# Neighbourhood attention: half of the probability maps turned by VectorE and sixteen on-chip transfers instead of TensorE

## The reference, cut to what matters

```python
def _na_mixer(h, hc, w_in, rpb, w_out, need_ctx_out):
    q, k, v, g = jnp.split(h @ w_in, 4, axis=-1)          # q scaled by 64 ** -0.5
    kc, vc = jnp.split(hc @ w_in[:, WIDTH:3 * WIDTH], 2, axis=-1)
    ...
    s_loc = s_loc + bias[None]        # rpb[:, dr, dc], 16 columns around each query, all 4 rows
    s_ctx = jnp.einsum('brqhd,bchd->bhrqc', q, kc)
    p = jax.nn.softmax(jnp.concatenate([s_loc.reshape(...), s_ctx], axis=-1), axis=-1)
    ...
    o = einsum(p_blk, vb) + einsum(p_ctx, vc)
    y = (o.reshape(b_, l_, WIDTH) * jax.nn.silu(g)) @ w_out
```

## Time and profile before

| | |
|---|---|
| median of three runs | 1814.95 us |
| the profiled execution: own time, span | 1815.61 us, 1813.8 us |
| PE, DVE, ACT, POOL busy, share of the span | 99%, 53%, 50%, 75% |
| granted TensorE clock, mean over the span | 0.998 |
| DMA: bytes, mean rate | 372.91 MB, 206 GB/s |
| busy from 300 to 350 us (attention): PE, DVE, ACT, POOL | 49.99, 33.29, 33.78, 22.94 us |
| DMA share from 300 to 350 us, rate | 0.71, 183 GB/s |

### The profile page before, as it was taken

One profiled execution on the slowest core, in us unless ns is written; L12 is line 12 of the kernel. 1 busy time (PEld: TensorE's weight loads), 2 busy tenths in 40 slices (PEclk: granted clock), 3 DMA queues, 4 the chain that ended last, 5 costly groups with the idle time before them and its releaser, 6 DMA issues.

```text
span 1813.8 us, 24988 instructions
## 1 busy us (share of the span) xinstructions
PE 1793.3 (99%) x9274; PEld 1477.5 (81%) x9274; DVE 954.2 (53%) x1756; ACT 901.5 (50%) x1329; POOL 1366.0 (75%) x568
## 2 busy tenths in 40 slices
PE   6999999999999999999999999999999999999999
PEld 5888888887889888887788888888888878888887
DVE  4673766778755524866653230713095876143152
ACT  3324424674455644456554644464445565555452
POOL 2624544559968898977689798969897867888885
PEclk9999999999999999999999999999999999999999
DMA  9863885749775775565665566567655666656663
GB/s 366 291 210 94 270 310 163 198 141 312 244 277 200 211 221 191 180 198 168 209 186 192 179 195 191 193 187 234 191 193 185 192 190 182 196 160 210 190 195 128
DMA packets 206457, 372.91 MB, mean 206 GB/s; under 512 B 33508, under 2 KB 59092, under 8 KB 205780
## 3 DMA queue, kind: packets, MB, share of 16 engines
q1 hardware_dynamic: 203328, 363.69, 63.5%
q10 hardware_dynamic: 3028, 7.86, 1.2%
HBM read 367.27 MB, written 9.28 MB: 208 GB/s over the span
## 4 chain that ended last, share of the span: by engine, by line
PE 97%; DVE 2%; DMA 0%; issue 0%; ACTq 0%; ACT 0%; POOL 0%; DVEq 0%
PE ps L1300 26%; PE ps L1302 25%; PE ps L1301 25%; PE ps L1426 3%; PE ps L1427 3%; PE ps L1428 3%; PE ps L1992 1%; PE ps L1993 1%; PE ps L1994 1%; PE ps L1348 1%; PE ps L1697 1%; PE ps L1918 1%; PE ps L1668 1%; PE ps L1678 1%; PE ps L1962 1%; PE ps L1558 1%
## 5 line engine op out<-in xcount | busy, mean ns | idle before, releaser
L659 POOL TENSOR_TENSOR w_lo<-raw,w_hi 128x1024 fp32r<-128x1024 f32 x556 | 1347.1, 2461 | 397.4 <-ACT w_hi L697 376.2
L1300 PE MATMUL ps<-w_hi,act_rows_r 128*128 128x512 f32 x2064 | 814.8, 395 | 3.2 <-POOL w_lo L659 3.1
L1302 PE MATMUL ps<-w_hi,act_rows_r 128*128 128x512 f32 x2064 | 805.2, 390 | 0.0
L1301 PE MATMUL ps<-w_lo,act_rows_r 128*128 128x512 f32 x2064 | 804.6, 390 | 0.0
L697 ACT ACTIVATE w_hi<-raw 128x1024 fp32r<-128x1024 f32 x556 | 571.1, 1058 | 371.0 <-DMA raw<-in_ffn_w_up 100.8
L1300 PEld LDWEIGHTS ps<-w_hi,act_rows_r 128*128 128x128 f32 x2064 | 388.2, 188 | 90.4 <-issue 9.1
L1302 PEld LDWEIGHTS ps<-w_hi,act_rows_r 128*128 128x128 f32 x2064 | 388.0, 188 | 82.0
L1301 PEld LDWEIGHTS ps<-w_lo,act_rows_r 128*128 128x128 f32 x2064 | 388.4, 188 | 77.7
L2647 DVE STREAM_TRANSPOSE ps<-proj 32x256 f32<-32x256 f32 (+1 forms) x384 | 166.5, 434 | 6.5
L2628 DVE TENSOR_TENSOR proj<-proj,ps 128x1024 f32<-128x1024 f32 (+1 forms) x18 | 20.4, 1132 | 252.2 <-PE ps L1302 247.9
L1426 PE MATMUL ps<-act_rows_r,w_hi 128*128 128x512 f32 (+1 forms) x288 | 101.3, 352 | 0.0
(11 more groups left out here) (245 smaller groups left out, 1554.0 us busy)
## 6 DMA issues: line engine op xcount, KB each, us to landing
raw<-in_w_in SPq DMA_DIRECT2D x120, 512.0 KB, 3.9
raw<-in_ffn_w_gate SPq DMA_DIRECT2D x88, 512.0 KB, 4.4
raw<-in_ffn_w_up SPq DMA_DIRECT2D x88, 512.0 KB, 4.4
raw<-in_ffn_w_down SPq DMA_DIRECT2D x88, 512.0 KB, 4.2
proj<-in_ada_w SPq DMA_DIRECT2D x39, 512.0 KB, 7.9
pt<-in_ada_w SPq DMA_DIRECT2D x38, 512.0 KB, 6.4
raw<-in_pool_w_in SPq DMA_DIRECT2D x32, 512.0 KB, 7.3
raw<-in_na_w_in SPq DMA_DIRECT2D x32, 512.0 KB, 4.9
```

Of the source, the lines that this page charges most:

```text
L659: pool.tensor_tensor(w_lo[:, s, :], raw[:, s, :], w_hi[:, s, :].bitcast(F32), ALU.subtract).then_inc(lo_done, 1)
L1300: pe.matmul(o, h, hi, start=start, stop=False)
L1301: pe.matmul(o, h, lo, start=False, stop=False)
L1302: return pe.matmul(o, c, hi, start=False, stop=stop)
```

## The change

For the units 0, 2, 4, 6, 8 and 10 (`NA_SQUARED`) PE no longer transposes. DVE transposes the maps inside each 32x32 block (`turned`), and the blocks then still lie on the wrong partitions. `exchange` moves them: sixteen transfers from SBUF to SBUF, each of 32 partitions x 1 KB, eight issued by SP and eight by ACT, from a buffer of squares (in `pt` or `bias`, by turns) to one placed buffer in `proj`. PE waits for all sixteen (`na_placed`), and reads the placed maps in runs of 32 columns. The values of a squared unit come five rounds after its scores instead of three (`na_due`). ACT issues its eight in round u + 4, SP after the output-weight group of that time.

The bias is loaded raw: four DMAs for each pair of heads, each 64 partitions x one run of 219 numbers, into a window buffer in `proj`; POOL reads the overlapping windows, adds the mask and writes the bias where DVE reads it, in two instructions, and waits itself for DVE to have used the earlier bias. The first two pairs are loaded at group 12 of the stage's input weights instead of group 7. The relation tables are written in the first block of each layer's first feed-forward stage.

```diff
+NA_SQUARED = (0, 2, 4, 6, 8, 10)
...
         def na_out_bank(u):
-            return 2 if u < NA_UNITS - 3 else 4
+            return 3 if u == NA_SQUARED[-1] else 2 if u < NA_UNITS - 3 else 4
+        def na_due(i):
+            return [u for u in range(NA_UNITS - 1) if u + (5 if u in NA_SQUARED else 3) == i]
+        def na_placed_rows(dims, at=0, rows=slice(0, P)):
+            return free(proj[rows, 0:1], dims, CTX_RES + 2 * D + at)
+        def na_squares(u, dims, at=0, rows=slice(0, P)):
+            return free((bias if u // 2 % 2 else pt)[rows, 0:1], dims, 2048 * (u // 2 % 2) + at)
+        def exchange(queue, u, targets):
+            queue.wait_ge(dve_done, dve_s.count(("na_sq", u)))
+            if u:
+                queue.wait_ge(pe_done, pe_s.count(("na_out", u - 2)))
+            for kq in targets:
+                for q in range(4):
+                    queue.dma_start(na_placed_rows([[1, 256]], 256 * q, slice(32 * kq, 32 * kq + 32)),
+                                    na_squares(u, [[1, 256]], 256 * kq, slice(32 * q, 32 * q + 32))).then_inc(na_placed, 16)
...
# SP
             def load_bias(hp):
-                for h, t, rq in ((h, t, rq) for h in range(2) for t in range(NT) for rq in range(2)):
-                    src = bass.AP(na_rows.tensor, (2 * hp + h) * RPB_HEAD + (7 - 2 * t - rq) * RPB_C + 15,
-                                  [[NA_ROW - 1, GRID_W], [RPB_C, 4], [1, GRID_W]])
...
+                if hp >= 2:
+                    sp.wait_ge(bias_masked, hp - 1)
+                for h in range(2):
+                    for rq in range(2):
+                        src = bass.AP(na_rows.tensor, (2 * hp + h) * RPB_HEAD + (5 - rq) * RPB_C + 15, [[NA_ROW - 1, GRID_W], [1, RPB_SPAN]])
+                        sp.dma_start(bias_windows(hp, [[1, RPB_SPAN]], h * 256, slice(64 * rq, 64 * rq + 64)), src).then_inc(bias_in[hp % 2], 16)
...
             for j in range(8):
                 if j < 6:
-                    sp.wait_ge(dve_done, dve_s.count(("na_l", 2 * j + 1)))
                     load_bias(j + 2)
                 send(I["na_w_out"][0][j * P:(j + 1) * P, :], [[1, D]])
-                if j in (1, 3):
-                    keep_rel(j // 2)
+                if 2 * j - 2 in NA_SQUARED:
+                    exchange(sp, 2 * j - 2, (0, 1))
+            sp.wait_ge(na_placed, 256 * len(NA_SQUARED))
...
+                        if tables and pair == 0:
+                            keep_rel(l)
...
# POOL
             def masked(hp):
-                pool.wait_ge(bias_in[hp % 2], 128 * (hp // 2 + 1))
-                both = free(bias[:, 0:1], [[SEQ, 4], [1, SEQ]], (hp % 2) * 1024)
-                pool.tensor_tensor(both, both, free(na_mask[:, 0:1], [[0, 4], [1, SEQ]]), ALU.add).then_inc(bias_masked, 1)
+                pool.wait_ge(bias_in[hp % 2], 64 * (hp // 2 + 1))
+                if hp >= 2:
+                    pool.wait_ge(dve_done, dve_s.count(("na_l", 2 * hp - 3)))
+                for t in range(NT):
+                    last = pool.tensor_tensor(free(bias[:, 0:1], [[512, 2], [GRID_W, 4], [1, GRID_W]], (hp % 2) * 1024 + t * SEQ), ...
# ACT, round i
-                        if i >= 3:
+                        if i - 3 in NA_SQUARED:
+                            act.wait_ge(dve_done, dve_s.count(("na_sq", i - 3)))
+                        elif i >= 3:
                             act.wait_ge(pe_done, pe_s.count(("na_t", i - 3, 1)))
...
+                    if i - 4 in NA_SQUARED:
+                        exchange(act, i - 4, (2, 3))
...
+                        if u not in NA_SQUARED:      # the copy of the turned maps, u = i - 2
...
# PE
             def na_values(u):
-                pe.wait_ge(dve_done, dve_s.count(("na_pt", u, 0)))
-                pe.wait_ge(act_done, act_s.count(("na_pt", u, 1)))
+                if u in NA_SQUARED:
+                    pe.wait_ge(na_placed, 256 * (u // 2 + 1))
+                else:
+                    pe.wait_ge(dve_done, dve_s.count(("na_pt", u, 0)))
+                    pe.wait_ge(act_done, act_s.count(("na_pt", u, 1)))
...
+                        maps = na_placed_rows([[256, 4], [1, 32]], 32 * (4 * c + k)) if u in NA_SQUARED else pt[:, o:o + P]
...
-                    if i >= 2:
+                    due = na_due(i)
+                    for u in due[:-1]:
+                        na_values(u)
+                    if i >= 2 and i - 2 not in NA_SQUARED:
                         na_turned(i - 2)
-                    if i >= 3:
-                        na_values(i - 3)
+                    for u in due[-1:]:
+                        na_values(u)
...
# DVE
                 def turned(u):
+                    if u in NA_SQUARED:
+                        dve.wait_ge(act_done, act_s.count(("na_e", u, 1)))
+                        if u >= 4:
+                            dve.wait_ge(na_placed, 256 * (u // 2 - 1))
+                        dve.transpose(na_squares(u, [[32, 8], [256, 4], [1, 32]]),
+                                      na_rows_of(u, [[P, 8], [32, 4], [1, 32]])).then_inc(dve_done, dve_s.one(("na_sq", u)))
+                    else:                            # the copy as before
...
```

More of the change, by code:

```diff
@@ L508, in narrow @@
                                 x_made(sp, prev, 1, nb)
[L509 to L512, removed]
+                        if stage == "na_in" and g == 12:
+                            sp.wait_ge(scratch_in, 16)
+                            load_bias(0)
+                            load_bias(1)
                         if stage == "na_in" and g == 16:
@@ L662, in masked @@
             def masked(hp):
-                pool.wait_ge(bias_in[hp % 2], 128 * (hp // 2 + 1))
-                both = free(bias[:, 0:1], [[SEQ, 4], [1, SEQ]], (hp % 2) * 1024)
-                pool.tensor_tensor(both, both, free(na_mask[:, 0:1], [[0, 4], [1, SEQ]]), ALU.add).then_inc(bias_masked, 1)
+                pool.wait_ge(bias_in[hp % 2], 64 * (hp // 2 + 1))
+                if hp >= 2:
+                    pool.wait_ge(dve_done, dve_s.count(("na_l", 2 * hp - 3)))
+                for t in range(NT):
+                    last = pool.tensor_tensor(free(bias[:, 0:1], [[512, 2], [GRID_W, 4], [1, GRID_W]], (hp % 2) * 1024 + t * SEQ),
+                                              bias_windows(hp, [[256, 2], [RPB_C, 4], [1, GRID_W]], 2 * RPB_C * (1 - t)),
+                                              free(na_mask[:, 0:1], [[0, 2], [GRID_W, 4], [1, GRID_W]]), ALU.add)
+                last.then_inc(bias_masked, 1)
             pool.wait_ge(dve_done, dve_s.count(("first_gains", 0, 1)))
@@ L962, in na_layer @@
                         u = i - 2
[L963 to L967, removed]
+                        if u not in NA_SQUARED:
+                            act.wait_ge(pe_done, pe_s.count(("na_t", u, 1)))
+                            if u == 12:
+                                act.wait_ge(na_placed, 256 * 5)
+                            if u >= 2:
+                                act.wait_ge(pe_done, pe_s.count(("na_out", u - 2)))
+                            act.activation(pt[:, (u % 2) * 1024 + 512:(u % 2) * 1024 + 1024], ps[:, 7, :],
+                                           ACT.Copy).then_inc(act_done, act_s.one(("na_pt", u, 1)))
                         if i == NA_UNITS:
@@ L1696, in na_values @@
                         o = (u % 2) * 1024 + c * 512 + k * P
-                        last = pe.matmul(ps[c * HD:(c + 1) * HD, bank, 0:P], v, pt[:, o:o + P], start=k == 0, stop=k == 3)
+                        maps = na_placed_rows([[256, 4], [1, 32]], 32 * (4 * c + k)) if u in NA_SQUARED else pt[:, o:o + P]
+                        last = pe.matmul(ps[c * HD:(c + 1) * HD, bank, 0:P], v, maps, start=k == 0, stop=k == 3)
                 last.then_inc(pe_done, pe_s.one(("na_out", u)))
@@ L2438, in turned @@
                 def turned(u):
[L2439 to L2442, removed]
+                    if u in NA_SQUARED:
[5 more added lines that the diff above has]
+                    else:
+                        dve.wait_ge(pe_done, pe_s.count(("na_t", u, 0)))
+                        if u == 12:
+                            dve.wait_ge(na_placed, 256 * 5)
+                        if u >= 2:
+                            dve.wait_ge(pe_done, pe_s.count(("na_out", u - 2)))
+                        dve.tensor_copy(pt[:, (u % 2) * 1024:(u % 2) * 1024 + 512], ps[:, 6, :]).then_inc(dve_done, dve_s.one(("na_pt", u, 0)))
                     dve.wait_ge(act_done, act_s.count(("na_e", u, 1)))
@@ L2476, in gated @@
                     dve.wait_ge(pe_done, pe_s.count(("tp", "nag", 0, k)))
[L2477 removed]
+                    dve.wait_ge(dve_done, dve_s.count(("na_o", na_last_of(k))))
                     z = ps[:, NA_Z_BANK[k], :].rearrange("p (c n) -> p c n", c=2)
@@ L2490, in na_layer @@
                         dve.wait_ge(pe_done, pe_s.count(("na_s", i)))
-                        if i >= 3:
+                        if i >= 3 and i - 3 not in NA_SQUARED:
```

(7 more changed lines are left out.)

11 lines of the change are left out of this document (7 added, 4 removed).

## The result

The changed kernel takes 1823.98 us (median; 1822.71 to 1824.72) against 1814.75 us of the kernel before on the same chip: 1.0048 times as long, 95% interval 1.0035 to 1.0060. The forecast was 1811.1 us, faster, in a range of 1809.0 to 1817.0; the kernel came out 9.2 us slower than before, 12.9 us above the forecast. The profiled execution has a span of 1822.6 us where that of before had 1813.8.

The account below looks back on a forecast made before the run. The prediction took TensorE (PE) to bound the kernel, 97% of the span; -5.2 + 0.85 + 0.5 = -3.85 us brought the profiled 1815.61 to 1811.76, by the median 1811.1 us, range 1809.0 to 1817.0.

Parts of the forecast that it names:

- ACT: Step on ACT's queue: eight DMA issues in every even round from 4 to 14, 0.46 us apart, 3.7 us.
- The rest: Step on bias loads, GpSimd's mask, SP's waits and relation copies: nothing added; eight bias loads take 0.65 us of SP each.
- Arrival: Transfers at a squared unit's values: there at 5.85 us after the scores; 0.1 us charged to five units, 0.85 to the first.
- ACT's pair: ACT's work for a pair of units: 0.2 + 3.7 + 1.05 + 2.0 + 0.5 = 7.5 us of 7.95.
- the flight: Time from a transfer's last issue to its landing: 1.8 us, and 0.15 for the semaphore.
- Transposes: On PE, six of sixteen units lose eight transposes: 6 x 0.87 = 5.2 us saved.
- Waits for transfers: PE's waits at squared units' values: 0.85 us in the first and 0.5 over the five others.
- t = 6.0: PE reaches the values waiting for the transfers 6.0 us after the scores of the round four later end.
- DVE's transposition: DVE transposes 128x1024 within 32x32 blocks instead of a 0.68 us copy: 1.30 us by size, between 0.98 and 1.30.
- The third: Rival at PE's values: their wait costs more than the transposes, from a mean stall of 0.87 us; chance 0.09.
- The fourth: Rival on ACT: issues start only after its copy and exponentials; +6.4 us, 1821.3; chance 0.04.
- The fifth: Rival on SP's and ACT's queues: they issue strictly in turn, stall 2.45 us in six units; +9.5, 1824.4; chance 0.02.

Follow-up runs that it names:

- experiment 3: Changed kernel, all transfers made but none waited for; exchanged units' values read a constant matrix instead of the placed maps: 1822.63 us, ratio 1.0049.
- experiment 7: Kernel of experiment 4 with the write of the squares put ahead of the next weight load: 1815.04 us, ratio 0.9996.
- experiment 8: Kernel of experiment 7 with unit 12's copies no longer waiting for unit 10's values: 1812.86 us, ratio 0.9993.
- experiment 9: Kernel of experiment 8 with unit 0 left to TensorE's transposes, so five units exchanged: 1811.59 us, ratio 0.9979.
- experiment 4: Changed kernel with each exchange by way of DRAM, one write and four reads, all issued by SP: 1819.53 us, ratio 1.0023.
- experiment 6: Changed kernel, SP alone moving the squares in four transfers of 128 rows of 1 KB, blocks landing straight: 1815.08 us, ratio 1.0001.
- experiment 1: Changed kernel with no unit exchanged, raw bias runs and moved relation copies kept: 1815.01 us, ratio 1.000.
- experiment 10: Changed kernel, on-chip exchange over two queues kept, without unit 0 and with unit 12's copies freed: 1822.46 us, ratio 1.0035.
- experiment 2: Changed kernel with only SP's eight transfers of each exchange made and waited for, ACT issuing none: 1817.82 us, ratio 1.0022.
- experiment 11: Changed kernel with all sixteen transfers of each exchange issued by SP, none by ACT: 1850.97 us, ratio 1.0188.

## Why the prediction was wrong

**The step that failed** is in "ACT": "twelve issues on ACT's queue, first and last shown, come 0.46 us apart, so eight are 3.7 us". They are 0.6 us apart, and eight take 5.0 to 6.6 us. A row that says so was in the prediction: the bias loads of this very stage, 5.20 us for eight, which the section "The rest" read as 0.65 us each. The start-up issues were taken because they stood on ACT's queue; the engine was not what mattered (592 ns on SP, 614 to 620 on ACT). Why the start-up issues are shorter no run shows. With 5.0 us the prediction's own sums turn over. Arrival: 0.2 + 5.0 + 1.95 = 7.15 against 6.0, a stall of 1.15 in five units and 2.15 in the first, 7.9 us. ACT's pair: 0.2 + 5.0 + 1.05 + 2.0 + 0.5 = 8.75 us, more than the 7.95 it had. Both consequences are shown, the second by experiment 3. That 7.9 lies near the measured 6.8 is in part luck: the flight was too long in the sum (with 1.3 us in place of 1.95 a regular row gives a stall of 0.5, and unit 8 has 0.52), and two rows were longer than 5.3 us by single long issues, which the prediction had no term for.

**Two terms stood at nothing without a row.** That moving unit 10's values back by two rounds holds up unit 12's copies, which wait for them, is nowhere in the prediction; it cost 2.5 us (experiments 7 and 8). And the scores of round 4 were brought forward by 1.9 us without asking whether DVE's sums come forward too: they did not; PE waits 0.5 us there, and 0.2 us at a query tile before.

**The sum, term by term.** Transposes: -5.2 forecast, borne out (0.87 a unit in experiment 9). Waits for transfers: +1.35 forecast, +6.8 measured. Ends of the stage, not in the sum: +3.2. Clock after the long wait, not in the sum: +1.4. Small waits for DVE: +0.4. Together +6.6; the stage measured +7.5, and 0.9 us is not assigned, with eleven waits in the stage. The same remainder is 0.8, 0.8, 0.4 and 0.3 us in experiments 3, 4, 6 and 8, with nine, nine, four and two waits, so it seems to go with their number; what it is was not traced.

**What held.** The place and time at which PE asks (t = 6.0), DVE's transposition (1.23 us, inside 0.98 to 1.30), that bias runs and relation copies are about free (experiment 1; five other profiles, the changed kernel's and those of experiments 6, 7, 8 and 10, have a wait of 0.4 to 0.7 us for weights in the first feed-forward stage, two of them before the first relation copy is issued; its cause was not traced), and that ACT's first issues run beside its exponentials. The value products' reading in runs of 32 columns cost nothing: sixteen take 1.09 us at full clock, as in the earlier trace rows.

**The rivals.** The third, the price nearest to the truth in kind (values wait more than the transposes cost), "decides from a mean stall of 0.87 us"; the mean stall was 1.1, but it came from the issues, where the rival has a flight of some 2.6 us. The fourth, issues that start only behind ACT's copy and exponentials, is refuted: the first starts at 327.42, 0.1 us after the scores. What it comes near to is another thing, ACT's own later work held behind the last five issues. The fifth, two queues strictly in turn, is refuted by experiment 2 and by the rows after: each queue keeps 0.6 us while the other issues. The Trainium skill (Perfetto Trace Analysis, "DMA Instruction — HWDGE (DVE, Sync)") has an exclusive lock there; no run here shows one at this cadence.

**Rule and row on the issues.** The Trainium skill (DMA: Bandwidth & Descriptors, "Issuing engines are not separate DMA queues") says that the time to initiate a DMA is "usually small relative to the DMA itself". Here it is not: of the 1.9 us from issue to landing 0.6 are the issue, and eight issues take 5.0 us, 2.6 times as long as one transfer from issue to landing.

## What to carry to other kernels

Count a transfer's issue as an instruction of its engine, with a duration read from issues of the same stage and in a row, before its bytes or its flight: here a few large transfers beat many small ones, and the engine that computes on the path is better off issuing none. Where a buffer's last reader is moved later, list everything that waits on that reader's semaphore. When a queue carries a transfer on the path, put it ahead of the bulk load that nothing waits for yet.

## What the runs showed of the hardware

- The length of an issue hardly depends on its bytes: 32 rows of 1 KB 0.59 us, 128 rows of 1 KB 0.60 us. The placing from DRAM, 32 rows of four runs, took 0.43 us, and the 512 KB write 0.34 to 0.38 (experiments 4 and 8).
- Single issues take 1.2 to 2.1 us now and then, on either queue (the longest in experiment 10), also where only SP issues (1.39 and 1.42 us in experiment 2). What sets them off is open.
- Two DVE instructions with two operands in SBUF each took 3.45 us together beside GpSimd's work (experiment 2) and 0.75 without (experiment 6); in the kernel before, such a pair took as much as 5.02 us at 379.62, with GpSimd at work. That agrees with the Trainium skill (SBUF — State Buffer, "SBUF: two separate sides"), by which the port pair that the two share is an exclusive lock. In experiment 2 it cost 2.9 us of PE's time, in experiment 6 nothing, with the same code for both engines, because GpSimd's work fell at another time.
- The granted clock came down behind PE's longest waits: in the changed kernel after the one of 2.51 us and not after the one of 1.88, in experiment 11 after each of its six of 3.9 to 4.4 us. A wait's price is then more than its length, here by 1.4 us.
